# A fused two-block transformer step: the gate projection is spread over the attention steps, and a matmul sequence is grouped by shape

## The chip, the cores and the metric

The kernel runs on one NeuronCore of a Trainium2 chip. The metric is device time in microseconds for one execution, from start to end on that core. The engines named below are PE (TensorE, the matmuls; its weight loads are listed apart as PEld), ACT (ScalarE), DVE (VectorE), POOL (GpSimd) and SP (the queue that issues the weight DMAs).

## What is computed

Two transformer blocks run on 256 tokens of width 1024, all in fp32. The change touches only the mixing layer of the first block. Cut to what matters there:

```python
h = _rms_norm(x, mix_norm)
proj = h @ w_in                      # 256 x 1024 times 1024 x 3584
aq, ak, av, hq, hf, hi, hg = split(proj)      # each 512 wide
attn_out = _dilated_attention(rope(norm(aq)), rope(norm(ak)), av)   # 8 heads of 64
rec = _hgrn2(hq, hf, hi, lower_bounds)        # 4 heads of 128, chunks of 64 tokens
rec = _rms_norm(rec, hg_out_norm) * silu(hg)  # the gate
x = x + concat([attn_out, rec]) @ w_out
```

The recurrence's output for a chunk is a masked 128x128 product with its values plus the decayed queries times the state before the chunk: `(intra + inter)`.

## The kernel before, in words

Every matrix of weights is cut into blocks of 128 x 2048 floats (1 MB). SP streams them in the order of a list, `plan` (lines 190 to 245), into a ring of eight slots; a slot is loaded again once the block that lay in it is used. A block is then split into a high part (ACT, line 299, `act_split`) and a low part (DVE, line 307, `dve_split`), so that an fp32 product becomes three fp32r matmuls (`mm3`, line 180). There are four slots for high parts, so a block can be split only when the block four places earlier in the list has been used. Each engine runs one program in a fixed order that is written out by hand, and the engines meet through semaphores alone.

A projection to 512 columns by `pe_tok` (line 528) takes two blocks, its halves. Each half is 24 matmuls of 512 columns (two token tiles, four k tiles, three products) into two PSUM banks. The five such projections have the numbers 0 (aq), 1 (ak), 2 (av), 3 (hi, the recurrence's values) and 4 (hg, the gate). In the list and on PE they stand in the order 0, 1, 3, 4, 2. ACT empties the banks in `kept` (line 794): a copy for 3 and 2, a silu for 4.

Between the halves of projections 4 and 2 stand small matmuls of the recurrence: `pe_rec_head` (line 637, per head the score product and two transposes), `pe_rec_state` (line 652, a chunk's state), and the transposes of q and k, `pe_qk_turn` (line 691).

Then the attention loop (line 749) runs over steps 0 to 10. A head h passes through these stations: `pe_scores` (PE) in step h; `biased` (DVE, line 917: bias and maximum) in step h; `exps` (ACT, line 805) in step h; `scaled` (DVE, line 927: division by the sum) in step h+1; `pe_turn_p` (PE, line 712, three transposes) in step h+2; `turned_p` (ACT, line 813, the copy out of PSUM) in step h+2; `pe_pv` (PE, line 723) in step h+3; and for each pair of heads `values` on ACT and on DVE. `pe_rec_out` (line 664) writes the recurrence's outputs in step 4 for both token tiles; `squares` on ACT (line 827) reads them in step 6 for both token tiles, and `roots`, `means` and `gated` follow. After the loop come the first group of `w_out` (24 matmuls, into banks 2 to 5), `pe_rec_turn` (line 677), and the groups 1 to 3 of `w_out`. ACT and DVE split the block of `w_out` 3 after their loops (lines 870 and 1001).

Plain fp32 matmuls, as in the attention and the recurrence, appear in the trace as two records each, called passes below.

Of the kernel before, what the change touches and what calls it, by code (L numbers as in the profile page):

```python
# [11 lines left out]
ACT = mybir.ActivationFunctionType  # L12
# [7 lines left out]
SPLIT = 4  # L20
# [72 lines left out]
def build(nc, a):  # L93
    ctx = ExitStack()
    with ctx:
# [81 lines left out]
        def mm(e, out, l, r, start, stop, **kw):  # L177
            return e.matmul(out, l, r, start=start, stop=stop, **kw)  # L178
# [6 lines left out]
        def both(x, f):  # L185
            return [f(y) for y in x]
# [22 lines left out]
        plan_ffn("ffn1", a["ffn1_w13"], a["ffn1_w2"], GROUPS)  # L209
        plan_all("w_hf", a["w_hf"])  # L210
        plan_all("w_hq", a["w_hq"])
        for i in (0, 1, 3, 4, 2):
            plan_all(("w_tok", i), a["w_tok"][i])
        plan_all("w_out", a["w_out"])
        plan_ffn("ffn2", a["ffn2_w13"], a["ffn2_w2"], GROUPS)
# [8 lines left out]
        for i in range(2):  # L224
# [10 lines left out]
            first = len(plan)  # L235
# [292 lines left out]
        def pe_tok(e, name, b0, b1, fresh=None, between=None):  # L528
            for half in range(2):
                blk, W = weights(e, (name, half), k=4)  # L530
                for t, b in ((0, b0), (1, b1)):
                    for k in range(4):
                        if fresh and t == 0 and k % 2 == 0:
                            e.wait_ge(*xt_low.at(fresh, 2 * half + k // 2))
                        i = mm3(e, banks[b][:, :], both(XT3, lambda x: x[:, 4 * half + k, t * 128:t * 128 + 128]),
                                both(W, lambda x: x[:, k, :]), half == 0 and k == 0, half == 1 and k == 3)
                    if half == 1 and t == 0:
                        i.then_inc(*half_done.mark(name))
                i.then_inc(*used.mark(blk))
                if half == 0 and between:  # L540
                    between()
# [90 lines left out]
        rec_att, rec_state, rec_out, rec_turned = signal("rec_att", mix_pe), signal("rec_state", mix_pe), signal("rec_out", mix_pe), signal("rec_turned", mix_pe)  # L632
        qk_turned, att_z, p_turned, att_v = signal("qk_turned", mix_pe), signal("att_z", mix_pe), signal("p_turned", mix_pe), signal("att_v", mix_pe)

        last_tok = index[("w_tok", 2), 1]

        def pe_rec_head(e, h):
            P = banks[h % 2]
# [25 lines left out]
        def pe_rec_out(e):  # L664
            for tt in range(2):
                P = banks[1 - tt]
                e.wait_ge(*state_n.at(2 if tt else 1))
                for h in range(4):
                    hv = slice(h * 128, h * 128 + 128)
                    i = mm(e, P[:, hv], att8[:, 2 * h + tt, :], HI3[:, tt, hv], True, False, skip_group_check=True)  # L670
                    for c in (2 * tt, 2 * tt + 1):
                        if c:
                            i = mm(e, P[(c % 2) * 64:(c % 2) * 64 + 64, hv], E1h[:, h, c * 64:c * 64 + 64],
                                   prv[:, c - 1, h, :], False, c % 2 == 1, skip_group_check=True)
                i.then_inc(*rec_out.mark(tt))
# [10 lines left out]
                i.then_inc(*rec_turned.mark(hp))  # L686

        def turned_bank(i, gp):
            return banks[(2 if i else 6) + gp]

        def pe_qk_turn(e, i):
            q3 = qk[i].rearrange("p (t d) -> p t d", t=2)
            e.wait_ge(*roped.at(i, 1))
            for gp in range(2):
                e.wait_ge(*(tok_kept.at(4, gp) if i else qk_norm.at(1, gp)))
                for k in range(2):
                    for t in range(2):
                        g = 2 * gp + k
                        j = e.transpose(turned_bank(i, gp)[:, k * 256 + t * 128:k * 256 + t * 128 + 128],
                                        q3[:, t, g * 128:g * 128 + 128], ident)  # L700
                j.then_inc(*qk_turned.mark(i, gp))
# [21 lines left out]
        def pe_pv(e, h):  # L723
            P, p = banks[6 + h // 2 % 2], PT[h % NP]
            o_, hv = slice((h % 2) * 64, (h % 2) * 64 + 64), slice(h * 64, h * 64 + 64)
            e.wait_ge(*pt_kept.at(h))
            if h >= 4 and h % 2 == 0:
                e.wait_ge(*mix_low.at("pv", h // 2 - 2))
            mm(e, P[o_, 0:128], V3[:, 0, hv], p[:, 0:128], True, True)
            mm(e, P[o_, 128:256], V3[:, 0, hv], p[:, 128:256], True, False)  # L730
            mm(e, P[o_, 128:256], V3[:, 1, hv], p[:, 256:384], False, True).then_inc(*att_v.mark(h))

        def pe_mix(e):
            pe_proj(e, ("w_hf", 0), XT3, banks[0], "mix")
            pe_proj(e, ("w_hf", 1), XT3, banks[1])
            pe_proj(e, ("w_hq", 0), XT3, banks[2])
            pe_proj(e, ("w_hq", 1), XT3, banks[3])
            pe_tok(e, ("w_tok", 0), 4, 5)
            pe_tok(e, ("w_tok", 1), 6, 7)
            e.wait_ge(*forget.at(1))  # L740
            pe_tok(e, ("w_tok", 3), 0, 1)
            e.wait_ge(*q_dec.at(1))
            pe_tok(e, ("w_tok", 4), 2, 3, between=lambda: (pe_rec_head(e, 0), pe_rec_head(e, 1)))
            pe_rec_head(e, 2)
            pe_rec_head(e, 3)
            pe_qk_turn(e, 0)
            e.wait_ge(*qk_norm.at(0, 1))
            pe_tok(e, ("w_tok", 2), 4, 5, between=lambda: (pe_rec_state(e, 0), pe_qk_turn(e, 1)))
            for i in range(11):
                if i < 8:  # L750
                    pe_scores(e, i)
                if i < 2:
                    pe_rec_state(e, 1 + i)
                elif i == 4:
                    pe_rec_out(e)
                if 2 <= i <= 9:
                    pe_turn_p(e, i - 2)
                if i >= 3:
                    pe_pv(e, i - 3)
            e.wait_ge(*mix_low.at("pv", 1))  # L760
            pe_down(e, "w_out", XT3, range(1), 2)
            pe_rec_turn(e)
            e.wait_ge(*mix_low.at("pv", 3))
            pe_down(e, "w_out", XT3, range(1, 2), 2)
            e.wait_ge(*mix_low.at("rec", 1))
            pe_down(e, "w_out", XT3, range(2, 4), 2)

        def act_mix(e, c):
# [25 lines left out]
            def kept(i, b, buf, func):  # L794
                for t in range(2):
                    tok_done(e, ("w_tok", i), t)
                    e.activation(buf[:, t * 512:t * 512 + 512], banks[b + t][:, :], func).then_inc(*tok_kept.mark(i, t))
# [26 lines left out]
                e.wait_ge(*att_masked.at(h))  # L824
                e.copy(ksT[:, h * 256:h * 256 + 256], banks[h % 2][:, 256:512]).then_inc(*ks_kept.mark(h))

            def squares():
                for tt in range(2):
                    e.wait_ge(*rec_out.at(tt))
                    for h in range(4):  # L830
                        hv = slice(h * 128, h * 128 + 128)
                        i = e.activation(XN3[:, tt, hv], banks[1 - tt][:, hv], ACT.Square,
                                         accum_out=rss[:, 4 * tt + h:4 * tt + h + 1])
                i.then_inc(*rec_sq.mark())

            def roots():
                e.wait_ge(*rec_mean.at())
# [6 lines left out]
                                 scale=par("hgn")).then_inc(*mix_high.mark("rec", hp))  # L844
            act_split(e, c, index[("w_tok", 3), 0] + SPLIT)
            kept(3, 0, HI, ACT.Copy)
            act_split(e, c, index[("w_tok", 4), 0] + SPLIT)
            kept_head(0)
            kept_head(1)
            kept(4, 2, SHG, ACT.Silu)  # L850
            kept_head(2)
            kept_head(3)
            turned_qk(0, -0.125)
            act_split(e, c, index[("w_tok", 2), 0] + SPLIT)
            e.wait_ge(*rec_state.at(0))
            e.copy(prev[:, 0:512], banks[0][:, :]).then_inc(*state_0.mark())
            turned_qk(1, 1.0)
            kept(2, 4, V, ACT.Copy)
            for i in range(12):
                if i < 8:  # L860
                    exps(i)
                if 2 <= i <= 9:
                    turned_p(i - 2)
                if i >= 5 and i % 2:
                    values((i - 5) // 2)
                if i == 6:
                    squares()
                elif i == 8:
                    roots()
            act_split(e, c, last_tok + SPLIT)  # L870
            rec_xt()
            for g in range(3):
                act_split(e, c, index["w_out", g] + SPLIT)
# [1 line left out]
        def dve_mix(e, c):  # L875
# [82 lines left out]
                i.then_inc(*state_n.mark(n))  # L958

            def means():  # L960
                e.wait_ge(*rec_sq.at())
                e.tensor_scalar(rss, rss, 1.0 / 128, 1e-6, ALU.mult, ALU.add).then_inc(*rec_mean.mark())

            def gated():
# [16 lines left out]
            dve_split(e, c, index[("w_tok", 3), 0] + SPLIT)  # L981
            masked(0)
            masked(1)
            dve_split(e, c, index[("w_tok", 4), 0] + SPLIT)
            masked(2)
            masked(3)
            dve_split(e, c, index[("w_tok", 2), 0] + SPLIT)
            for i in range(12):
                if i < 8:
                    biased(i)  # L990
                if 1 <= i <= 8:
                    scaled(i - 1)
                if i >= 5 and i % 2:
                    values((i - 5) // 2)
                if i in (1, 2):
                    states(i)
                elif i == 7:
                    means()
                elif i == 9:
                    gated()  # L1000
            dve_split(e, c, last_tok + SPLIT)
            rec_xt()
            for g in range(2):
                dve_split(e, c, index["w_out", g] + SPLIT)
# [1490 lines left out]
```

## Time and profile before

| what | value |
|---|---|
| median of 3 runs | 1333.2 us (1331.91 to 1340.69) |
| the profiled execution's own time | 1335.28 us |
| its span in the trace | 1333.4 us |
| granted PE clock over the span | 0.983 of full speed |
| PE busy | 1269.5 us, 95% of the span |
| DVE, ACT, POOL busy | 612.2, 466.9, 205.6 us |
| chain that ended last | PE 89%, DVE 7%, ACT 2% |

The span is the time from the first to the last instruction in the trace; the time of the execution is 1.9 us more. The chain is followed back from the last instruction, at each step to what released it. An engine that is off this chain can be late without cost until another engine waits for it. The mixing layer lies between about 220 and 350 us of the span; the stretch that the change reorders lies between 270.56 and 333.51 us.

### The profile page before, as it was taken

How to read it: one execution, taken by the hardware profiler on the slowest of the kernel's cores; microseconds unless marked ns; L12 is line 12 of the kernel's file. 1: busy time of each engine (PE TensorE's matmuls, PEld its weight loads, DVE VectorE, ACT ScalarE, POOL GpSimd, SP SyncE). 2: the span in 40 equal slices, each digit the busy share in tenths (PEclk: the TensorE clock that was granted, in tenths of full speed). 3: DMA queues.
4: the chain of work that ended last, by engine and by line, in shares of the span. 5: the costliest groups of instructions: out<-in, count | busy, mean ns of one | idle time of the engine just before them, and what ended most of it. 6: DMA issues, size and time to landing. Idle time of an engine off the chain costs nothing.

```text
span 1333.4 us, 18498 instructions
## 1 busy us (share of the span) xinstructions
PE 1269.5 (95%) x7906; PEld 924.0 (69%) x7906; DVE 612.2 (46%) x816; ACT 466.9 (35%) x634; POOL 205.6 (15%) x207
## 2 busy tenths in 40 slices
PE   6999999998999999999899999997999899999995
PEld 6999997886799999888664444434898665444432
DVE  6644556845676764476731111117465651111114
ACT  5544344655446444325410101014676420001111
POOL 0000000410499990030000000000033000000000
PEclk9999999999999999989999999998999999999998
DMA  9555553540555555515599999996523399999992
GB/s 390 185 180 180 186 190 129 191 159 28 174 185 187 190 189 167 190 41 188 200 373 419 422 421 420 421 421 248 169 92 127 127 350 395 421 421 421 421 420 113
DMA packets 47750, 338.33 MB, mean 254 GB/s; under 512 B 5296, under 2 KB 5296, under 8 KB 7728
## 3 DMA queue, kind: packets, MB, share of 16 engines
q1 hardware_dynamic: 45936, 330.53, 64.6%
q10 hardware_dynamic: 1728, 6.55, 1.3%
q8 instruction: 66, 1.08, 0.3%
q14 instruction: 20, 0.16, 0.0%
HBM read 336.02 MB, written 1.05 MB: 253 GB/s over the span
## 4 chain that ended last, share of the span: by engine, by line
PE 89%; DVE 7%; ACT 2%; issue 1%; DMA 1%; SPq 0%; ACTq 0%; DVEq 0%
PE pb L178 88%; DVE halves L307 1%; DVE SM L1476 1%; DVE Xs L1487 1%; DMA ring<-in_ffn_w 1%; PE pb L1916 1%; DVE Xs L403 0%; DVE Xs L1482 0%; DVE Xs L405 0%; DVE XN L340 0%; ACT halves L299 0%; DVE p L1655 0%; DVE XN L349 0%; DVE Xs L1500 0%; DVE XTl L392 0%
## 5 line engine op out<-in xcount | busy, mean ns | idle before, releaser
L178 PE MATMUL pb<-XTh,halves 128*128 128x256 f32 x1856 | 338.8, 283 | 6.9 <-DVE XTl L392 4.9
L307 DVE TENSOR_TENSOR halves<-ring,halves 128x2048 fp32r<-128x2048 f32 (+1 forms) x122 | 285.1, 2352 | 130.2 <-ACT halves L299 129.9
L178 PEld LDWEIGHTS pb<-XTh,halves 128*128 128x128 f32 x1856 | 291.2, 192 | 9.1 <-issue 4.1
L178 PE MATMUL pb<-XTl,halves 128*128 128x256 f32 x928 | 262.3, 283 | 0.0
L299 ACT CAST halves<-ring 128x2048 fp32r<-128x2048 f32 (+1 forms) x122 | 227.4, 1874 | 83.4 <-PE pb L178 79.4
L178 PE MATMUL pb<-ring,gather 128*64 128x512 f32 x832 | 189.8, 598 | 3.2 <-DVE gather L2054 1.7
L178 PEld LDWEIGHTS pb<-XTl,halves 128*128 128x128 f32 x928 | 177.8, 192 | 0.9
L178 PE MATMUL pb<-halves,XTh 128*128 128x512 f32 x512 | 160.5, 395 | 5.0 <-DVE halves L307 3.0
L178 PEld LDWEIGHTS pb<-ring,gather 128*64 128x64 f32 x832 | 57.5, 137 | 109.2 <-issue 105.0
L2050 DVE TENSOR_TENSOR slots_h<-slots_silu,pb 128x256 f32<-128x256 f32 x32 | 13.5, 421 | 229.3 <-ACT slots_silu L2012 229.3
L178 PEld LDWEIGHTS pb<-halves,XTh 128*128 128x128 f32 x512 | 95.6, 190 | 26.0 <-DVE halves L307 6.0
L178 PE MATMUL pb<-halves,HTh 128*128 128x512 f32 x352 | 110.8, 396 | 0.0
L178 PE MATMUL pb<-halves,XTl 128*128 128x512 f32 x256 | 100.0, 391 | 0.0
L2058 DVE SCALAR_TENSOR_TENSOR slots_y<-pb,SM,slots_y 128x512 fp32r<-128x512 f32 x32 | 24.0, 751 | 117.4 <-ACT slots_y L2024 117.4
L178 PEld LDWEIGHTS pb<-places,XN 128*128 128x128 f32 x512 | 60.1, 193 | 23.4 <-issue 23.4
L1679 POOL TENSOR_TENSOR p<-p,CO 128x256 f32<-128x256 f32 x16 | 14.9, 959 | 392.1 <-DVE p L1659 392.1
L2024 ACT ACTIVATE slots_y<-pb,SM 128x512 fp32r<-128x512 f32 x32 | 22.0, 688 | 152.2 <-PE pb L178 152.2
L178 PEld LDWEIGHTS pb<-halves,HTh 128*128 128x128 f32 x352 | 64.8, 188 | 14.1
L178 PE MATMUL pb<-ring,slots_ht 128*64 128x512 f32 x320 | 72.9, 597 | 0.0
L178 PE MATMUL pb<-halves,HTl 128*128 128x512 f32 x176 | 69.6, 395 | 0.0
L178 PE MATMUL pb<-places,XN 128*128 128x128 f32 x512 | 65.8, 283 | 1.6 <-ACT gate_sig L1840 1.6
L2016 ACT COPY slots_ht<-pb 128x256 f32<-128x256 f32 x32 | 11.9, 372 | 138.4 <-PE pb L1916 138.0
(348 smaller groups left out, 1389.4 us busy)
## 6 DMA issues: line engine op xcount, KB each, us to landing
ring<-in_moe_w SPq DMA_DIRECT2D x144, 1024.0 KB, 13.6
ring<-in_ffn_w SPq DMA_DIRECT2D x66, 1024.0 KB, 5.0
extra<-in_moe_w SPq DMA_DIRECT2D x48, 1024.0 KB, 14.6
ring<-in_w_tok SPq DMA_DIRECT2D x10, 1024.0 KB, 5.0
ring<-in_ple_gate SPq DMA_DIRECT2D x8, 1024.0 KB, 4.9
ring<-in_w_out SPq DMA_DIRECT2D x4, 1024.0 KB, 4.9
ring<-in_ab_out SPq DMA_DIRECT2D x4, 1024.0 KB, 4.9
ring<-in_sb_v SPq DMA_DIRECT2D x4, 1024.0 KB, 22.8
```

What stands on the lines that cost most here:

```text
L178: return e.matmul(out, l, r, start=start, stop=stop, **kw)
L299: e.copy(split_of(n)[0], raw_of(n)).then_inc(*high.mark(n))
L307: e.tensor_tensor(l, raw_of(n), h.bitcast(F32), ALU.subtract).then_inc(*low.mark(n))
L1476: s = e.bn_stats(st4[:, t, h, :], X3[:, t, h * 512:h * 512 + 512])
L1487: e.scalar_tensor_tensor(x, x, r, GB[:, 1024:2048], ALU.mult, ALU.add).then_inc(*x_new.mark("norm", i, t))
L1679: e.tensor_tensor(diag(LL[h % 8]), diag(LL[h % 8]), strict2, ALU.mult).then_inc(*sb_strict.mark(h))
L1916: j = e.transpose(banks[7][:, c * 128:c * 128 + 128], HM[n][:, c * 128:c * 128 + 128], ident)
L2016: e.copy(HT4[p % 2][:, 2 * n:2 * n + 2, :], banks[7][:, 0:256]).then_inc(*s.h_kept.mark(p, n))
L2024: e.activation(Y[h][0], down_bank(p, h)[:, :], ACT.Copy, scale=slot_gate[:, p:p + 1]).then_inc(*s.y_high.mark(p, h))
L2050: e.tensor_tensor(HM[n], SL[n], banks[5 + n][:, 256:512], ALU.mult).then_inc(*s.mul.mark(p, n))
L2058: e.scalar_tensor_tensor(Y[h][1], down_bank(p, h)[:, :], slot_gate[:, p:p + 1], Y[h][0].bitcast(F32), ALU.mult, ALU.subtract).then_inc(*s. ...
```

## The change

The list of blocks and PE's order have the values' projection (2) before the gate's (4). The gate's 48 matmuls are no longer issued by `pe_tok` but by a new function, `pe_gate`, in four portions: 8 before `pe_rec_state(0)`, then 13, 13 and 14 in the attention steps 0, 1 and 2. They write banks 6 and 7. The transposes of q use banks 2 and 3 as those of k do. In `pe_rec_out` the four heads' masked products are issued first, then the products with the state. It is called in step 3 in place of 4. ACT applies silu in step 3, takes the squares of the first token tile in step 3 and of the second in step 8, and the roots in step 10. The splits of later blocks move into steps 1 and 3 on ACT and 0, 1 and 3 on DVE. The last two `pe_pv` are issued after the first group of `w_out`, which now has a wait for each bank.

```diff
-        for i in (0, 1, 3, 4, 2):
+        for i in (0, 1, 3, 2, 4):
             plan_all(("w_tok", i), a["w_tok"][i])
...
-                    i = mm(e, P[:, hv], att8[:, 2 * h + tt, :], HI3[:, tt, hv], True, False, skip_group_check=True)
+                    mm(e, P[:, hv], att8[:, 2 * h + tt, :], HI3[:, tt, hv], h == 0, False, skip_group_check=True)
+                for h in range(4):
+                    hv = slice(h * 128, h * 128 + 128)
                     for c in (2 * tt, 2 * tt + 1):
...
         def turned_bank(i, gp):
-            return banks[(2 if i else 6) + gp]
+            return banks[2 + gp]
...
-                e.wait_ge(*(tok_kept.at(4, gp) if i else qk_norm.at(1, gp)))
+                e.wait_ge(*(qkt_kept.at(0, gp) if i else q_dec.at(1)))
...
-            if h >= 4 and h % 2 == 0:
-                e.wait_ge(*mix_low.at("pv", h // 2 - 2))
+            if h % 2 == 0:
+                e.wait_ge(*(tok_kept.at(4, h // 2) if h < 4 else mix_low.at("pv", h // 2 - 2)))
...
+        def pe_gate(e, first, stop):
+            for n in range(first, stop):
+                half, t, k, part = n // 24, n // 12 % 2, n // 3 % 4, n % 3
+                blk, W = index[("w_tok", 4), half], both(split_of(index[("w_tok", 4), half]), lambda x: x.rearrange("p (k n) -> p k n", k=4))
+                if n % 24 == 0:
+                    e.wait_ge(*low.at(blk))
+                if half == 0 and k == 0 and part == 0:
+                    e.wait_ge(*qk_norm.at(1, t))
+                i = mm(e, banks[6 + t][:, :], XT3[part == 2][:, 4 * half + k, t * 128:t * 128 + 128], W[part == 1][:, k, :],
+                       half == 0 and k == 0 and part == 0, half == 1 and k == 3 and part == 2)
+                if n % 24 == 23:
+                    i.then_inc(*used.mark(blk))
+                elif n == 35:
+                    i.then_inc(*half_done.mark(("w_tok", 4)))
...
-            e.wait_ge(*q_dec.at(1))
-            pe_tok(e, ("w_tok", 4), 2, 3, between=lambda: (pe_rec_head(e, 0), pe_rec_head(e, 1)))
+            e.wait_ge(*qk_norm.at(0, 1))
+            pe_tok(e, ("w_tok", 2), 4, 5, between=lambda: (pe_rec_head(e, 0), pe_rec_head(e, 1), pe_qk_turn(e, 0)))
             pe_rec_head(e, 2)
             pe_rec_head(e, 3)
-            pe_qk_turn(e, 0)
-            e.wait_ge(*qk_norm.at(0, 1))
-            pe_tok(e, ("w_tok", 2), 4, 5, between=lambda: (pe_rec_state(e, 0), pe_qk_turn(e, 1)))
-            for i in range(11):
+            pe_qk_turn(e, 1)
+            pe_gate(e, 0, 8)
+            pe_rec_state(e, 0)
+            for i in range(10):
                 if i < 8:
                     pe_scores(e, i)
-                if i < 2:
-                    pe_rec_state(e, 1 + i)
-                elif i == 4:
+                if i in (1, 2):
+                    pe_rec_state(e, i)
+                elif i == 3:
                     pe_rec_out(e)
+                if i < 3:
+                    pe_gate(e, 8 + 13 * i, 21 + 13 * i if i < 2 else 48)
                 if 2 <= i <= 9:
                     pe_turn_p(e, i - 2)
-                if i >= 3:
+                if 3 <= i < 9:
                     pe_pv(e, i - 3)
             e.wait_ge(*mix_low.at("pv", 1))
-            pe_down(e, "w_out", XT3, range(1), 2)
+            pe_down(e, "w_out", XT3, range(1), 2, free=lambda b: att_max.at(6 + b) if b < 2 else pt_kept.at(4 + b))
+            pe_pv(e, 6)
+            pe_pv(e, 7)
             pe_rec_turn(e)
```

On ACT, in order (DVE's splits stand beside them in steps 0, 1 and 3):

```diff
-            act_split(e, c, index[("w_tok", 4), 0] + SPLIT)
+            act_split(e, c, index[("w_tok", 2), 0] + SPLIT)
             kept_head(0)
             kept_head(1)
-            kept(4, 2, SHG, ACT.Silu)
+            turned_qk(0, -0.125)
+            kept(2, 4, V, ACT.Copy)
             kept_head(2)
             kept_head(3)
-            turned_qk(0, -0.125)
-            act_split(e, c, index[("w_tok", 2), 0] + SPLIT)
+            turned_qk(1, 1.0)
             e.wait_ge(*rec_state.at(0))
             e.copy(prev[:, 0:512], banks[0][:, :]).then_inc(*state_0.mark())
-            turned_qk(1, 1.0)
-            kept(2, 4, V, ACT.Copy)
+            act_split(e, c, index[("w_tok", 2), 1] + SPLIT)
             for i in range(12):
                 if i < 8:
                     exps(i)
+                if i == 1:
+                    act_split(e, c, index[("w_tok", 4), 0] + SPLIT)
+                elif i == 3:
+                    kept(4, 6, SHG, ACT.Silu)
+                    act_split(e, c, index[("w_tok", 4), 1] + SPLIT)
+                    squares(0)
                 if 2 <= i <= 9:
                     turned_p(i - 2)
                 if i >= 5 and i % 2:
                     values((i - 5) // 2)
-                if i == 6:
-                    squares()
-                elif i == 8:
+                if i == 8:
+                    squares(1)
+                elif i == 10:
                     roots()
-            act_split(e, c, last_tok + SPLIT)
             rec_xt()
```

## Rows read from the trace of the kernel before

**Rows 1.** The page: busy time of each engine, and the chain that ended last.
```profile
PE 1269.5 (95%) x7906; PEld 924.0 (69%) x7906; DVE 612.2 (46%) x816; ACT 466.9 (35%) x634; POOL 205.6 (15%) x207
...
PE 89%; DVE 7%; ACT 2%; issue 1%; DMA 1%; SPq 0%; ACTq 0%; DVEq 0%
```

**Rows 2.** Timeline of PE: start us, us, operation; in brackets the idle before.
```profile
270.56 0.61 PE L178 MATMUL pb<-halves,XTh 128*128 128x512 f32 x2
...
276.00 0.60 PE L178 MATMUL pb<-p,p 128*128 128x128 f32 x4
...
298.13 2.83 PE L178 MATMUL pb<-p,p 64*128 64x128 f32 x28
301.97 0.55 PE L720 MATMUL pb<-CO,p 128*128 128x128 f32 x3 [1.01 <-DVE p L933]
...
304.21 0.55 PE L720 MATMUL pb<-CO,p 128*128 128x128 f32 x3 [0.85 <-DVE p L933]
304.92 7.99 PE L178 MATMUL pb<-p,p 128*64 128x128 f32 x50 [0.17 <-ACT p L817]
312.85 0.55 PE L720 MATMUL pb<-CO,p 128*128 128x128 f32 x3
...
314.97 0.55 PE L720 MATMUL pb<-CO,p 128*128 128x128 f32 x3
...
319.80 0.87 PE L178 MATMUL pb<-p,p 128*64 128x128 f32 x6
...
323.11 1.45 PE L178 MATMUL pb<-p,p 128*64 128x128 f32 x6 [1.88 <-ACT p L817]
324.57 0.90 PE L720 MATMUL pb<-CO,p 128*128 128x128 f32 x3
...
327.12 0.73 PE L178 MATMUL pb<-halves,XTh 128*128 128x512 f32 x2
...
333.51 0.70 PE L178 MATMUL pb<-halves,XTh 128*128 128x512 f32 x2
```

**Rows 3.** Busy time by stretch: engines in order, PEclk, DMA share, GB/s.
```profile
306.57:312.85 6.28, 6.28 (x42) 3.94 (x41) 1.28 (x8) 1.72 (x7) 0.00 (x0) 1.00 0.00 0
...
323.10:327.12 4.02, 4.00 (x21) 3.10 (x21) 1.91 (x8) 2.85 (x6) 0.00 (x0) 0.58 0.00 0
```

**Rows 4.** Timeline of PE's weight loads in attention step 4.
```profile
305.72 0.52 PEld L178 LDWEIGHTS pb<-p,p 64*128 64x128 f32 x4 [0.17 <-issue]
...
308.91 0.61 PEld L178 LDWEIGHTS pb<-p,p 128*128 128x128 f32 x4 [0.17 <-issue]
309.69 0.62 PEld L178 LDWEIGHTS pb<-p,p 128*128 128x128 f32 x6 [0.17 <-issue]
```

**Rows 5.** Busy time by stretch, one microsecond after PE's last wait.
```profile
324.00:325.00 1.00, 0.99 (x5) 0.59 (x4) 0.52 (x2) 1.00 (x1) 0.00 (x0) 0.50 0.00 0
```

**Rows 6.** Timeline of ACT: the loop's start, head 2, head 4.
```profile
298.85 1.28 ACT L808 ACT_TABLE_LOAD   x1
300.14 0.40 ACT L808 ACTIVATE p<-p,SM 128x128 f32<-128x128 f32 x1
...
303.52 0.40 ACT L808 ACTIVATE p<-p,SM 128x128 f32<-128x128 f32 x1 [1.52 <-DVE SM L924]
...
304.41 0.46 ACT L817 COPY p<-pb 128x384 f32<-128x384 f32 x1
...
307.35 0.40 ACT L808 ACTIVATE p<-p,SM 128x128 f32<-128x128 f32 x1
```

**Rows 7.** Groups of ACT's instructions, 276 to 333.51 us: count, busy us, mean ns.
```profile
L299 ACT CAST halves<-ring 128x2048 fp32r<-128x2048 f32 x4 | 7.6, 1910 | 5.8 <-PE pb L178 5.8
...
L797 ACT ACTIVATE p<-pb 128x512 f32<-128x512 f32 x4 | 2.4, 598 | 5.9 <-PE pb L178 5.9
...
L832 ACT ACTIVATE XN<-pb 128x128 f32<-128x128 f32 x8 | 2.1, 291 | 0.0
```

**Rows 8.** Timeline of DVE: the low part of one block.
```profile
292.65 2.29 DVE L307 TENSOR_TENSOR halves<-ring,halves 128x2048 fp32r<-128x2048 f32 x1 [2.31 <-ACT halves L299]
```

More of the change, by code:

```diff
@@ L633, in build @@
         qk_turned, att_z, p_turned, att_v = signal("qk_turned", mix_pe), signal("att_z", mix_pe), signal("p_turned", mix_pe), signal("att_v", mix_pe)
-        last_tok = index[("w_tok", 2), 1]
+        last_tok = index[("w_tok", 4), 1]
         def pe_rec_head(e, h):
@@ L825, in kept_head, with squares @@
                 e.copy(ksT[:, h * 256:h * 256 + 256], banks[h % 2][:, 256:512]).then_inc(*ks_kept.mark(h))
[L827 to L834, printed above, removed]
+            def squares(tt):
+                e.wait_ge(*rec_out.at(tt))
+                for h in range(4):
+                    hv = slice(h * 128, h * 128 + 128)
+                    i = e.activation(XN3[:, tt, hv], banks[1 - tt][:, hv], ACT.Square,
+                                     accum_out=rss[:, 4 * tt + h:4 * tt + h + 1])
+                i.then_inc(*rec_sq.mark(tt))
             def roots():
@@ L960, in means @@
             def means():
-                e.wait_ge(*rec_sq.at())
+                e.wait_ge(*rec_sq.at(1))
                 e.tensor_scalar(rss, rss, 1.0 / 128, 1e-6, ALU.mult, ALU.add).then_inc(*rec_mean.mark())
@@ L983, in dve_mix @@
             masked(1)
-            dve_split(e, c, index[("w_tok", 4), 0] + SPLIT)
+            dve_split(e, c, index[("w_tok", 2), 0] + SPLIT)
             masked(2)
             masked(3)
-            dve_split(e, c, index[("w_tok", 2), 0] + SPLIT)
             for i in range(12):
@@ L994, in dve_mix @@
                     values((i - 5) // 2)
-                if i in (1, 2):
-                    states(i)
-                elif i == 7:
+                if i == 0:
+                    dve_split(e, c, index[("w_tok", 2), 1] + SPLIT)
+                elif i == 1:
+                    states(1)
+                    dve_split(e, c, index[("w_tok", 4), 0] + SPLIT)
+                elif i == 2:
+                    states(2)
+                elif i == 3:
+                    dve_split(e, c, index[("w_tok", 4), 1] + SPLIT)
+                elif i == 9:
                     means()
-                elif i == 9:
+                elif i == 10:
                     gated()
-            dve_split(e, c, last_tok + SPLIT)
             rec_xt()
```

## The prediction, made before the changed kernel was run

> **What bounds the kernel now.** I read the page first. PE is busy 95% of the span and holds 89% of the chain that ended last [rows 1]: a change pays only if it takes work or idle time from PE, and work that is only moved on PE pays nothing. The changed code lies between 270.56 us (first half of projection 4) and 333.51 us (group 1 of `w_out`), 62.95 us or 4.7% of the span, so the whole effect has to be found there. PE's timeline of this stretch [rows 2] shows four things that are not work at full speed.
>
> 1. Waits at the loop's start: 1.01, 0.85 and 0.17 us, while heads 0 and 1 go through DVE and ACT and PE has nothing else to issue.
> 2. `pe_rec_out`, from 306.57 to 312.85 us: 6.28 us for 40 passes [rows 3]. Its weight loads show why. A head with 4 passes takes 0.78 us from start to start, a head with 6 also (309.69 less 308.91), and each time 0.17 us of nothing stand ahead of the next head [rows 4]. Each head alternates between a product that fills 128 columns of the array and products that fill 64.
> 3. One wait of 1.88 us at 323.11, for the copy of head 5's transposed probabilities on ACT, which stands behind all eight squares in ACT's queue.
> 4. A low clock behind that wait: 0.58 granted from 323.10 to 327.12 [rows 3], and 0.50, the 1.2 GHz level, in a whole microsecond of it [rows 5]. Six passes of `pe_pv` take 1.45 us there and 0.87 us before it, three transposes 0.90 and 0.55 [rows 2].
>
> **The change part by part.** I follow PE's order with these durations up to the start of `w_out` group 1, and keep ACT's and DVE's queues beside it.
>
> *Projections swapped.* Both have two halves of 24 matmuls, 5.44 us each (276.00 less 270.56, [rows 2]), 0.227 us a matmul. The swap costs nothing on PE. The transposes of q move in between the halves; their rotation by POOL was needed earlier than that in neither kernel, since q's projection is the first of the five.
>
> *The gate's 48 matmuls.* 10.9 us of PE work, moved and not removed. With about 0.11 us a pass, two heads take 1.3, the transposes of q or k 0.8, a chunk's state 1.1: from 276.0 on, 1.3 + 0.8 + 5.4 + 1.3 + 0.8 + 1.8 (8 gate matmuls) + 1.1 bring PE to step 0 at about 288.6 us (298.13 before). Steps 0 to 2 add 40 gate matmuls (9.1), three scores, two states and the changes of shape (4.0): the gate is issued at 301.6. PE doesn't idle until then: heads 0 and 1 have three portions of about 3 us as cover. This removes the 2.03 us of item 1. The cover matters, since ACT now casts a block (1.91 us, [rows 7]) and loads Exp's table (1.28, [rows 6]) before head 0's exponentials; these start at about 292.4, head 0's transposes only at 301.6. The cost: the portions are a shape of their own between the 64-row products of scores and states, which stood together (28 passes in one run at 298.13). Three more changes of shape each way at 0.17 us at most [rows 4], less where the next load is hidden: I take 0.5 us, bounds 0 and 1.0.
>
> *`pe_rec_out` grouped.* 16 changes of shape become 4. With 0.17 us a change and two passes of 128 columns at 0.11, a head of 0.78 us leaves 0.22 us for its four 64-column passes; pairs at different columns seem to overlap, as heads with 4 and 6 passes take the same. Grouped: token tile 0 is 8 + 8 passes and 2 changes, 2.1 us; tile 1 is 8 passes, 8 pairs and 2 changes, 2.3. Sum 4.4, so 1.9 us saved. Bounds: 0 if the order within a bank doesn't matter, 2.3 if all is hidden.
>
> *ACT in step 3.* This is the new place to be late. After head 3's exponentials (scores at 302.1, 1.63 us later as for head 4, 305.72 to 307.35, [rows 4, 6], and 0.89 us long, 303.52 to 304.41) ACT is at 304.6. Behind them stand: Silu's table 1.28, two silus 1.1 (0.60 each, overlapping a little, [rows 7]), the cast of `w_out` 3 1.85, four squares 1.0 (half of the 2.0 us from 319.65 on; the group row has 2.1), and only then the copy of head 1's transposes: ready to start at 309.8, done at 310.3. PE asks for it, in `pe_pv(1)`, after 301.6 + 0.5 + 0.85 + 4.4 + 0.5 + 0.8 + 0.85 + 0.5 = 310.0 (transposes 0, scores 3, outputs, transposes 1, `pe_pv(0)`, scores 4, transposes 2; the loop's period of 2.12 us, 312.85 to 314.97, [rows 2], is made of 0.48, 0.80 and 0.85). Wait: 0.3 us. DVE stands behind ACT's cast with its own 2.29 us [rows 8], so head 4's maximum comes at 311.7; Exp's table is back at 311.5. Heads 3 and 4 are late by this, and PE waits 0.6 us more at `pe_turn_p(3)`, 0.3 at 6 (heads 5 to 7 follow DVE and ACT closely) and 0.7 at 7.
>
> *Squares and last values.* With the squares halved and the second half behind head 6's copy, the 1.88 us of item 3 go. The last two `pe_pv` stand behind 24 matmuls of `w_out`, which hide their copies; then 0.1 us is left before group 1. The four bank waits of `w_out` 0 cost nothing: bank 4 is asked for 1.4 us into it. Without the wait of 1.88 us the low clock goes as well: 0.6 + 0.35 us in the two rows of item 4, 1.0 us in all; bounds 0 (it falls anyway) and 1.0.
>
> *DMA.* The loads released by the two halves of the block that now comes last go out at about 295 and 301.6 (290.5 and 298.1 before); the DMA engines are idle from 306 to 327 [rows 3], and these loads are for ffn2, after 358 us. Nothing.
>
> *Sum.* 2.03 + 1.88 idle, 1.9 grouping, 1.0 clock, less 0.5 for shapes and 2.0 for new waits: 4.3 us. Followed step by step, group 1 of `w_out` starts at 329.2 in place of 333.51. Behind it the order is the same and PE bound, so the gain stays. Against the profiled time of 1335.28 that is 1331.0; that execution stands 2.1 us above the median of 1333.2, and I give the prediction for the median: **1329.0 us**.
>
> One dependence is worth saying: ACT's queue sets `pe_pv(1)`. If grouping saved nothing, PE would come 1.9 us later and not wait there, and the end would be only 0.9 us later. If PE were faster still, ACT would eat it.
>
> **A rule of the Trainium skill against the trace.** The table load of 1.28 us at 298.85 is followed by its exponential at 300.14, 1.29 us later, with nothing between [rows 6]. The Trainium skill (ScalarE: Activation LUTs, What ACT_TABLE_LOAD costs) has a drain of 1.38 us beside the load, 2.66 us for each switch. By it the sum would be 1.8 us in place of 4.3. The trace doesn't agree.
>
> **The rivals.**
> - *Forecast* (0.66): 1329.0, own range 1326.5 to 1331.5.
> - *No new waits* (0.10): ACT and DVE keep up in step 3. Then 6.3 us are gained: 1326.9. For it: item 1's removal leaves heads ahead. Against: the queue in step 3 is counted from rows.
> - *Table switches at double price* (0.08): the change adds one switch (Exp, Silu, Exp, Sqrt for Silu, Exp, Sqrt) and moves two into step 3, between head 3 and head 4. If the load's own 1.28 us stood once more behind each of them, head 1's copy would be done at 311.6 and head 4's exponentials would start at 314.1, 2.4 us later than forecast; two of these reach PE: a gain of 2.0 us, 1331.2. The load at 298.85 speaks against it [rows 6]; it might hold where more is in flight on ACT before the load.
> - *Slower, by the clock* (0.05): the new waits lie close together from 310 to 320 us. A wait of 1.88 us did drop the clock; 1.01 and 0.85 didn't. If it fell at 310 and stayed at 1.2 GHz to the end of `w_out` 0, some 9 us of attention work would take 1.65 times as long (1.45 for 0.87) and 5.4 us of matmuls twice, less 2 us of waits that vanish in it: +9.3, net 5 us slower, 1338. It decides from about 10 us of low clock on (4.3 + 2 over 0.65); before it lasted about 4.
> - *The change doesn't do what it says* (0.05): the gate's operands come late and PE waits inside the portions. Then item 1's gain and cover are gone and some 1 us stays: 1332. The split of the gate's second block ends at about 280 (DVE) and is needed at 295, so 15 us speak against it.
> - *Something outside the stretch* (0.06), either sign, such as another place of code or data in memory: nothing in the profile shows it; half of it is for more than 13 us faster and half for more than 13 us slower.
>
> **The numbers.** What a measurement of this kernel can tell from no change is about 1%, 13 us; only the last case gets there. So faster 0.03, within 1% 0.94, slower 0.03. The range takes the forecast's own, the rivals from 1326.9 to 1332, and the spread of a median of runs that themselves go from 1331.91 to 1340.69: 1325.0 to 1334.0.
>
> **What would show it.** PE without a wait over 0.3 us until the gate is issued; `pe_rec_out` at 4.4 us with few gaps ahead of its weight loads; ACT without idle between head 3's exponentials and head 1's copy; no wait near 1.9 us before `w_out`, and the clock at 1.00 through the loop; `w_out` 1 at about 329 us. Wrong would be: `pe_rec_out` still above 5.5, a gap behind a table load, or a wait over 1.5 us at `pe_pv(1)` with the clock falling behind it.

## The result, and the profile after

| | kernel before | changed kernel |
|---|---|---|
| median, executions in turns | 1340.41 us (1331.23 to 1343.65, 21 executions) | 1328.08 us (1326.45 to 1331.29, 21 executions) |
| span of the profiled execution | 1333.4 us | 1326.1 us |
| the stretch, from the first `pe_rec_head` to group 1 of `w_out`, in the profiled execution | 57.51 us | 53.62 us |

The ratio of the times is 0.9922, 95% interval 0.9906 to 0.9939. The forecast was 1329.0, range 1325.0 to 1334.0: the time lies in it. But the kernel before was itself at 1340.41 in this larger set, and not at the 1333.2 of the three executions shown: the difference is 12 us, almost three times the 4.3 that were forecast. Much of what follows is about these 8 us.

The changed stretch first, as PE's timeline of the changed kernel has it (start us, us, operation, idle before it; the rows without `halves` from the loop's third step to head 3's value product, those with a wait behind them, and the marks at both ends).

```profile
277.38 0.61 PE L178 MATMUL pb<-p,p 128*128 128x128 f32 x4
...
304.11 0.49 PE L722 MATMUL pb<-CO,p 128*128 128x128 f32 x3
304.53 5.14 PE L178 MATMUL pb<-p,p 64*128 64x128 f32 x44
309.60 0.55 PE L722 MATMUL pb<-CO,p 128*128 128x128 f32 x3
310.07 1.72 PE L178 MATMUL pb<-p,p 128*64 128x128 f32 x10
311.72 0.55 PE L722 MATMUL pb<-CO,p 128*128 128x128 f32 x3
312.80 1.72 PE L178 MATMUL pb<-p,p 128*64 128x128 f32 x10 [0.53 <-ACT p L838]
314.92 0.55 PE L722 MATMUL pb<-CO,p 128*128 128x128 f32 x3 [0.40 <-DVE p L957]
315.64 1.72 PE L178 MATMUL pb<-p,p 128*64 128x128 f32 x10 [0.18 <-ACT p L838]
...
321.59 0.87 PE L178 MATMUL pb<-p,p 128*64 128x128 f32 x6 [0.17 <-ACT p L838]
322.98 0.55 PE L722 MATMUL pb<-CO,p 128*128 128x128 f32 x3 [0.51 <-DVE p L957]
...
331.00 0.73 PE L178 MATMUL pb<-halves,XTh 128*128 128x512 f32 x2
```

This execution began 1.38 us later (277.38 for the 276.00 of [rows 2]), so durations are compared, not times. The waits of 1.01, 0.85 and 1.88 us in [rows 2] are gone. Scores 3 and the recurrence's outputs take 5.07 us together (304.53 to 309.60), so the outputs some 4.2, where they took 6.28 [rows 3]. In place of the old waits stand 0.53, 0.40, 0.18, 0.17 and 0.51 us, 1.8 in all, the first two of them at the places that the forecast named: `pe_pv(1)` and `pe_turn_p(3)`.

ACT's timeline of the changed kernel in step 3, which answers to [rows 6]:

```profile
306.96 0.19 ACT L831 ACTIVATION_READ_ACCUMULATOR p<-p,SM 128x1 f32 x1
307.16 1.28 ACT L818 ACT_TABLE_LOAD   x1
308.45 1.08 ACT L818 ACTIVATE p<-pb 128x512 f32<-128x512 f32 x2
309.43 1.90 ACT L299 CAST halves<-ring 128x2048 fp32r<-128x2048 f32 x1
311.21 0.29 ACT L852 ACTIVATE XN<-pb 128x128 f32<-128x128 f32 x1
...
312.23 0.51 ACT L838 COPY p<-pb 128x384 f32<-128x384 f32 x1
312.76 1.28 ACT L829 ACT_TABLE_LOAD   x1
314.24 0.40 ACT L829 ACTIVATE p<-p,SM 128x128 f32<-128x128 f32 x1 [0.19 <-DVE SM L948]
```

ACT has no idle time from head 3's exponentials to the copy of head 1's transposes at 312.23, for which PE waits. The silus follow 1.29 us after the start of their table load, at once behind it; the work of the second load waited 0.19 us for DVE (head 4's maximum). The drain of 1.38 us that the Trainium skill has beside the load (ScalarE: Activation LUTs, What ACT_TABLE_LOAD costs) is not here either.

The rest of the difference of 7.3 us between the two spans lies 230 us further on, in the small products of the state-space layer. The kernel before, by stretch (busy time of PE, PEld, DVE, ACT, POOL, then PEclk, DMA share, GB/s), and the first matmul behind that layer (the row's last part but one is the start of the first and of the last):

```profile
565.00:568.00 3.00, 3.00 (x76) 3.00 (x71) 0.00 (x0) 0.00 (x0) 0.00 (x0) 0.60 0.42 172
568.00:571.00 3.00, 3.00 (x64) 3.00 (x64) 0.00 (x0) 0.00 (x0) 0.00 (x0) 0.50 0.03 5
...
577.00:580.00 3.00, 3.00 (x23) 2.18 (x16) 2.73 (x5) 1.15 (x2) 1.97 (x2) 0.63 0.00 0
...
L178 PE MATMUL pb<-places,XN x512: 275/275/422, 676.6 to 1280.4; 128*128 128x128 f32 x171
```

The changed kernel:

```profile
565.00:568.00 3.00, 3.00 (x100) 2.87 (x96) 0.08 (x1) 0.00 (x0) 0.00 (x0) 1.00 0.03 5
568.00:571.00 3.00, 3.00 (x70) 2.59 (x63) 2.93 (x7) 1.15 (x2) 0.00 (x0) 1.00 0.02 5
...
L178 PE MATMUL pb<-places,XN x512: 275/275/561, 669.2 to 1273.1; 128*128 128x128 f32 x171
```

From group 1 of `w_out` to that matmul it is 343.1 us before (676.6 less 333.51) and 338.2 after. So the spans differ by 3.9 us from the changed stretch and 4.9 from a spell at half the clock that this execution of the kernel before had and this one of the changed kernel had not, less 1.4 for the later start, which is itself a low clock (0.78 granted from 15 to 20 us of the span, where the trace of the kernel before has 1.00). These 4.9 us are in no line that was changed, and the next section shows that the 12 us between the medians are yet another sum.

### The profile page after: what moved, and what is told of

Read it like the earlier page. It is cut to its first block, busy times and chain, and to the rows that moved or that the text cites. A ratio compares the mean times of both kernels' runs of the same rounds, so it can differ in the third digit from the quotient of the medians.

```text
span 1326.1 us, 18501 instructions
## 1 busy us (share of the span) xinstructions
PE 1262.8 (95%) x7906; PEld 920.1 (69%) x7906; DVE 612.2 (46%) x816; ACT 468.6 (35%) x635; POOL 206.0 (16%) x207
## 4 chain that ended last, share of the span: by engine, by line
PE 88%; DVE 8%; ACT 1%; issue 1%; DMA 1%; SPq 0%; ACTq 0%; DVEq 0%
PE pb L178 87%; DVE halves L307 1%; DVE SM L1505 1%; DVE Xs L1516 1%; DMA ring<-in_ffn_w 1%; PE pb L1945 1%; DVE Xs L403 0%; DVE Xs L1511 0%; ACT halves L299 0%; DVE Xs L405 0%; DVE XN L340 0%; DVE p L1684 0%; PE pb L364 0%; DVE Xs L1529 0%; DVE rot L1404 0%
```

## The experiments

Two theories stood against each other. The **local** one is the forecast's: waits and passes in the changed stretch, at full clock, are all there is. The **clock** one: most of the difference is how often and how long PE's clock is at 1.2 GHz. All the medians below are of 7 to 12 executions, taken in turns with the kernel before, which had a median of 1340.3 to 1340.5 each time. They come from three chips. Such a median depends on how many executions happen to fall into the long group, as the first run shows, so the lists of times are compared too.

**The kernel before again** (no edit).

> The kernel before, unchanged, once more with a trace. Two theories on the 7.3 us between the two traces' spans. Local theory: what the change does in its own stretch (270.56 to 333.51 us) is all there is, about 4 us; then the executions of the kernel before differ among themselves for no reason that its trace shows, and the ratio to itself is 1.000 within 0.3%. Clock theory: about 4 us come from the stretch and the rest from PE's clock later on: in the trace of before it was at 1.2 GHz from about 565 to 579 us (the small products of the state-space layer), in the trace after it was not. Then executions of this kernel fall into groups (about 1332 and 1341), and the mean granted clock of an execution is lower in the long group, by some 0.005 to 0.01.

Measured: median 1334.95, for 1340.34 of the 35 executions of the same kernel beside it, ratio 0.9984 (0.9955 to 1.0012). Five of its 12 executions at 1340.4 to 1342.1 us with a granted clock of 0.977 or 0.978, seven at 1331.8 to 1335.3 with 0.983 to 0.987. Of the 35, 22 lay at 1339.3 to 1344.0 (0.976 to 0.981) and 13 at 1328.8 to 1335.4 (0.985 to 0.991); nothing between. The one that was profiled is of the long group, span 1340.0. Its PE timeline:

```profile
277.39 0.60 PE L178 MATMUL pb<-p,p 128*128 128x128 f32 x4
...
303.35 0.55 PE L720 MATMUL pb<-CO,p 128*128 128x128 f32 x3 [1.01 <-DVE p L933]
...
305.59 0.90 PE L720 MATMUL pb<-CO,p 128*128 128x128 f32 x3 [0.84 <-DVE p L933]
306.43 13.92 PE L178 MATMUL pb<-p,p 128*64 128x128 f32 x50
320.27 0.90 PE L720 MATMUL pb<-CO,p 128*128 128x128 f32 x3
...
336.04 0.55 PE L720 MATMUL pb<-CO,p 128*128 128x128 f32 x3
...
338.38 0.73 PE L178 MATMUL pb<-halves,XTh 128*128 128x512 f32 x2
...
344.75 0.71 PE L178 MATMUL pb<-halves,XTh 128*128 128x512 f32 x2
```

and its stretches:

```profile
304.00:315.00 11.00, 10.16 (x34) 6.22 (x34) 5.06 (x27) 3.68 (x14) 0.00 (x0) 0.53 0.01 2
315.00:325.00 10.00, 10.00 (x41) 6.14 (x41) 0.71 (x5) 0.54 (x2) 0.00 (x0) 0.50 0.00 0
325.00:335.00 10.00, 10.00 (x36) 6.76 (x35) 4.13 (x21) 6.59 (x33) 0.00 (x0) 0.50 0.01 2
...
335.00:340.00 5.00, 4.80 (x29) 3.73 (x29) 2.63 (x11) 4.13 (x7) 0.00 (x0) 0.95 0.01 2
```

The clock falls at the second of the two waits at the loop's start and stays at 1.2 GHz for some 30 us. It is back at 335.4 us, among the same small passes of the loop (the transposes at 336.04 take 0.55 us again), 3 us before the first matmul of `w_out` at 338.38. The wait of 1.88 us near the end is not in this execution; behind the second of the two waits PE waits only once more, for 0.20 us at 337.58. The 50 passes that took 7.99 us in [rows 2] take 13.92. The stretch is 67.36 us (344.75 less 277.39) for 57.51. So the 9 us between the groups are here, in the stretch that was changed, and the execution that the forecast was read from was one without the fall. This also turns the question: the state-space layer had no spell in this execution, and the clock theory's place was wrong.

**Grouping alone**, in the kernel before.

```diff
-                    i = mm(e, P[:, hv], att8[...], HI3[...], True, False, skip_group_check=True)
+                    mm(e, P[:, hv], att8[...], HI3[...], h == 0, False, skip_group_check=True)
+                for h in range(4):
+                    hv = slice(h * 128, h * 128 + 128)
```

> The kernel before with the recurrence's outputs grouped by shape and nothing else. Forecast's step: the outputs take 4.4 us for 6.28, and as every engine waits for PE there, group 1 of w_out starts 1.9 us earlier relative to the first half of projection 4 (62.95 us before, 61.1 expected). Rival: the saving becomes a longer wait before the copy of head 5 (1.88 us before), because ACT's eight squares are what that wait is made of; then under 0.5 us is left. Times of whole executions: 1331 or 1339, by the group that they fall into; under the clock theory both groups still occur.

```profile
304.98 5.94 PE L178 MATMUL pb<-p,p 128*64 128x128 f32 x50 [0.17 <-ACT p L819]
310.85 0.55 PE L722 MATMUL pb<-CO,p 128*128 128x128 f32 x3
...
321.12 0.87 PE L178 MATMUL pb<-p,p 128*64 128x128 f32 x6 [1.88 <-ACT p L819]
322.58 0.55 PE L722 MATMUL pb<-CO,p 128*128 128x128 f32 x3 [0.59 <-DVE p L935]
```

In PE's timeline the same 50 passes take 5.87 us to the next row (310.85 less 304.98) and took 7.93 (312.85 less 304.92, [rows 2]): 2.06 us for 12 changes of shape fewer, 0.17 each. The Trainium skill says that a change of tiling mode, not of tile, drains the engine (TensorEngine Tiling (Array Packing), Key Properties); the trace agrees in so far as each change costs time, 0.17 us; a drain as such is no row of it. 1.3 us of it reach the end of the stretch (56.21 us), for the 1.9 expected, in the main since a wait of 0.59 appears at head 7; the rival's 0.5 is out too. The median is 1335.16 with groups at 1329.2, 1334 to 1336.5 and 1338. The three at 1338, with a granted clock of 0.980 or 0.981, are probably the long group made 2 to 3 us shorter; none of them has a trace.

**The changed kernel without the grouping** (the same edit undone).

> The changed kernel with the recurrence's outputs in the old order within each token tile. Forecast's step: the outputs take 6.3 us, but the stretch grows only by 0.9 us, since ACT's queue in step 3 is what PE waits for behind them (the waits at head 1's and head 3's transposes shrink). Rival: no such cover, the stretch grows by the full 1.9 us. Clock theory: whole executions stay in the group of the changed kernel (1327 to 1332) if the gate's move is what keeps the clock up, and two groups come back if the outputs' grouping is.

Measured: stretch 54.37 us, 0.75 more than the changed kernel's, though the outputs took 2.05 us longer. No wait at heads 1 and 3 is left; they were what ACT's queue had cost. The cover is as forecast. Median 1329.71, but 3 of 12 executions at 1333.0 to 1335.5, where the changed kernel has none above 1331.43 in 28. There is no group at 1340, so the grouping is not what the changed kernel needs to be rid of it; what the three are has no trace.

**The changed kernel with squares and last values put back.**

```diff
-                    squares(0)                      # step 3
-                if i == 8:
-                    squares(1)
-                elif i == 10:
+                if i == 6:
+                    squares(0)
+                    squares(1)
+                elif i == 8:
                     roots()
...
-            pe_down(e, "w_out", XT3, range(1), 2, free=...)
-            pe_pv(e, 6)
-            pe_pv(e, 7)
+            pe_down(e, "w_out", XT3, range(1), 2)   # the values in steps 9 and 10
```

> The changed kernel with three things put back: squares of both token tiles in step 6 and roots and gating in steps 8 and 9 as before, and the last two value products ahead of w_out. Forecast's step: the wait near 1.9 us before head 5's value product comes back and the stretch grows by 1.6 us, by 2.6 if the clock falls behind the wait as it did before. Rival: heads are so far ahead after the gate's move that ACT's squares are hidden: under 0.5 us. Clock theory: if a low clock here is what leads to the low clock 240 us later, long executions (about 1338) come back.

```profile
315.06 0.55 PE L722 MATMUL pb<-CO,p 128*128 128x128 f32 x3 [1.00 <-DVE p L955]
...
322.99 0.87 PE L178 MATMUL pb<-p,p 128*64 128x128 f32 x6 [1.43 <-ACT p L836]
324.46 0.55 PE L722 MATMUL pb<-CO,p 128*128 128x128 f32 x3 [0.59 <-DVE p L955]
```

The stretch is 55.23 us, 1.61 more. PE's timeline has the wait at head 5 back, at 1.43 us. The clock did not fall here, and no long execution came (1329.5 to 1334.3): the wait near the end is not what makes the group at 1340. Nor does every pair of waits of this length bring the clock down: here are 1.00 and 1.43 us, 6.5 us apart, at a granted clock of 1.00 throughout.

**The two waits filled**, in the kernel before: one matmul that nobody reads ahead of the transposes of heads 0 and 1.

```diff
+                if i in (2, 3):
+                    mm(e, banks[7][:, :], ident, CO[:, 0:512], True, True)
                 if 2 <= i <= 9:
                     pe_turn_p(e, i - 2)
```

> The kernel before, with one matmul whose result nobody reads (0.9 us, into bank 7) put ahead of the transposes of head 0 and of head 1, where PE waits 1.01 and 0.85 us. Clock theory, as the traces now suggest it: these two waits are what lets PE's clock fall at about 305 us in most executions of the kernel before, and it then stays at 1.2 GHz for some 30 us. With the waits filled the group at 1340 us is gone; the median falls from 1340 to 1332 or 1333, with no useful work moved. Rival: the fall has another cause (the 64-row and 64-column products of the loop load the array too little), then the filling changes nothing: more than half of the executions stay above 1338, and the median is that of the kernel before.

```profile
298.00:304.00 6.00, 6.00 (x42) 4.17 (x40) 2.60 (x14) 3.74 (x10) 0.00 (x0) 1.00 0.51 176
304.00:315.00 11.00, 10.83 (x64) 6.63 (x65) 5.15 (x27) 3.77 (x15) 0.00 (x0) 1.00 0.00 1
```

Measured: median 1333.93, ratio 0.9960 (0.9936 to 0.9985), a little above the 1332 or 1333 expected, with a stretch of 57.57 us, which is the 57.51 of [rows 2]. Not one of 12 executions is at 1340; eleven lie at 1329.3 to 1337.2, one at 1354 (clock 0.933, not explained; the kernel before has one such too among its 25 beside it, at 1449.8 with 0.840). The traced one, at 1337.1, has the spell in the state-space layer. Adding useless work to PE (each filler takes 1.12 us in the trace) took 6.6 us off the median. This shows that the long group needs these two waits: with the same passes behind them, and no waits, it doesn't come. What it does not tell apart: a filler takes the idle time away and also puts a matmul of 512 columns among small ones, and either could be what holds the clock up. So do the gate's portions in the changed kernel.

**The gate's matmuls all ahead of the loop**, in the changed kernel.

```diff
-            pe_gate(e, 0, 8)
+            pe_gate(e, 0, 48)
             pe_rec_state(e, 0)
...
-                if i < 3:
-                    pe_gate(e, 8 + 13 * i, 21 + 13 * i if i < 2 else 48)
```

> The changed kernel with all 48 gate matmuls ahead of the recurrence's state 0 and none in the attention steps. Theory (the spread portions are cover): ACT's cast and table load now stand open, PE waits about 3 us at head 0's transposes and again about 3 us within the recurrence's outputs, the stretch grows by 7.5 us at full clock, and the clock falls behind these waits for a long spell, which adds up to 10 us: 1336 at the best, 1345 to 1350 in most executions. Rival (the gate's place is of no matter, the rest of the change carries the gain): the stretch grows by 2 us, the waits of the kernel before, 1330.

```profile
298.00:304.00 6.00, 3.19 (x29) 2.88 (x26) 4.18 (x13) 5.36 (x10) 0.00 (x0) 0.97 0.46 168
304.00:310.00 6.00, 6.00 (x23) 4.75 (x23) 4.71 (x14) 3.09 (x8) 0.00 (x0) 0.50 0.00 0
310.00:315.00 5.00, 3.57 (x34) 2.71 (x33) 2.00 (x11) 3.89 (x9) 0.00 (x0) 0.96 0.00 0
```

Measured: stretch 60.31 us, 6.7 more than the changed kernel's, for the 7.5 expected, with waits of 2.81, 0.52, 0.91 and 1.43 us as the largest; median 1337.83. The spread portions are the cover, though the second wait, within the outputs, is 0.52 us and not about 3. And the long spell did not come: the clock fell at 304 and was back at 310.4, before the second token tile's outputs (310.88). Nine executions are at 1334.5 to 1338.2 and three at 1342.9 to 1346.4; I had expected most above 1345. A fall is not yet a long spell; something else keeps the clock low.

**The same with the outputs in the old order.**

> The changed kernel with the gate's matmuls all ahead of the loop, and with the recurrence's outputs in the old order. With the gate first and the outputs grouped, PE's clock fell behind a wait of 2.81 us but was back at full speed some 6 us later, while in the long executions of the kernel before it stayed low for about 30 us. Theory G (the alternation of 128 and 64 columns is what keeps the clock low once it has fallen): the spell now lasts to the end of the loop and most executions come to 1345 us or more. Rival R (how long the spell lasts has to do with what follows the waits, not with the order within the outputs): 1 to 2 us longer than with the outputs grouped, median 1339 to 1340.

```profile
304.00:310.00 6.00, 5.98 (x18) 3.67 (x19) 4.72 (x13) 3.09 (x8) 0.00 (x0) 0.50 0.00 0
310.00:315.00 5.00, 5.00 (x20) 3.01 (x20) 2.04 (x11) 3.88 (x9) 0.00 (x0) 0.50 0.00 0
315.00:325.00 10.00, 10.00 (x39) 6.27 (x38) 3.56 (x8) 5.77 (x16) 0.00 (x0) 0.50 0.00 0
325.00:335.00 10.00, 10.00 (x36) 6.76 (x35) 4.22 (x22) 4.44 (x17) 0.00 (x0) 0.50 0.01 2
```

Behind the same wait of 2.81 us the clock now stays low to the end of the loop; the stretch is 69.65 us. Median 1343.16, nine of 12 at 1342.3 to 1350.4 where the grouped one had three. The median is a little under what I wrote (1345 or more), but the rival's 1339 to 1340 is out. So the order of the outputs probably has a hand in how long the clock stays down: one trace of each is not a law, and the share of executions (9 of 12 for 3 of 12, on two chips) is the firmer part. It can't be all of it. In this trace and in that of the kernel before again the clock stays at 0.50 through the loop steps behind the outputs, whose order no edit touched; and here too it comes back ahead of `w_out`: the last transposes, at 337.36 us, take 0.79 in place of 0.90, and `w_out` starts at 337.90. What brings the clock back is open.

**Both in the kernel before**: waits filled and outputs grouped, gate where it was.

> The kernel before with the two waits filled by a matmul each and the outputs grouped, the gate left where it was. If the clock's fall behind the waits is the greater part of the change's gain and the grouping adds 2 us to it, the median is 1330 to 1332, some 2 us under the filled kernel and 1 to 3 above the changed one, and no execution is above 1338. Theory G gives the same; a median above 1334 would say that filling and grouping don't add.

Measured: median 1330.41, ratio 0.9952 (0.9925 to 0.9979). Eight of 12 lie at 1327.8 to 1331.6, four at 1336.5 to 1337.0; the trace is of one of the four, its stretch is at full clock (54.81 us), and it has the spell in the state-space layer that the first trace had. The wait before head 5's value product stands in this stretch too, with 1.87 us, and the clock did not fall behind it; in the other three traces with that wait (the first one, grouping alone, waits filled) it did. The medians of the two kernels are 12.3 us apart; these two small edits bring 9.9 in this set.

**A lighter queue**: in the changed kernel the split of `w_out` 3 goes back behind the loops, the first squares go to the end of step 5, and head 7's transposes stand inside group 0 of `w_out`.

```diff
-                    act_split(e, c, index[("w_tok", 4), 1] + SPLIT)   # step 3; on DVE too
-                    squares(0)
+                if i == 5:
+                    squares(0)
...
+                        if hook and k == 0 and 2 * t + h == 1:
+                            hook()                                   # pe_turn_p(e, 7)
```

> The changed kernel with three waits attacked: the split of w_out 3 goes back behind the loops, the squares of the first token tile go from step 3 to the end of step 5, and the transposes of head 7 are issued inside w_out 0, after its first three matmuls. Theory (ACT's queue in step 3 and the thin steps at the end are what PE still waits for, 0.53 + 0.40 + 0.18 + 0.17 + 0.51 us): the stretch shrinks by 0.9 us and these waits go; whole executions 0.9 us shorter than the changed kernel, in the same groups. Rival: waits only move on along the heads, as DVE and ACT follow PE closely; under 0.3 us.

```profile
275.91 0.61 PE L178 MATMUL pb<-p,p 128*128 128x128 f32 x4
...
318.81 0.87 PE L178 MATMUL pb<-p,p 128*64 128x128 f32 x6 [0.17 <-ACT p L840]
...
327.70 0.72 PE L178 MATMUL pb<-halves,XTh 128*128 128x512 f32 x2
```

These are the stretch's two ends and the one wait that is left in it. It takes 51.79 us, 1.83 less than the changed kernel's 53.62: twice what I expected, since all but 0.17 of the 1.8 us of waits went. The 0.9 us expected of whole executions didn't come: median 1329.37 of 7, beside 1329.36 of 7 for the changed kernel. Seven executions of each that reach from 1322.95 to 1332.62 are too few to tell, as spells elsewhere move one by more.

**The changed kernel again**, on the same chip.

> The changed kernel once more, beside the others on the same chip. Both theories: median 1326.5 to 1331, no execution above 1336; granted clock 0.985 or more in all.

Measured: median 1329.36, 1326.8 to 1331.4, granted clock 0.986 to 0.989, stretch 53.62 us to the hundredth.

## Why the prediction was right, and where it was not

- *The two waits at the start.* Forecast 2.03 us gained, PE busy until the gate is issued: so it was, no wait in the first three steps.
- *Changes of shape in the outputs.* Forecast 1.9 us saved; grouping alone saves 2.06. That grouping alone would reach the end with only 0.9 us in the changed kernel: 0.75.
- *ACT in step 3.* The wait was forecast at `pe_pv(1)` with 0.3 us and at `pe_turn_p(3)` with 0.6; it was 0.53 and 0.40. Together with the later ones 2.0 was forecast and 1.8 found.
- *Changes of shape between the gate's portions.* Put at 0.5 us with a bound of 1.0; this term was mis-sized. PE is busy 53.55 of the stretch's 57.51 us before and 51.72 of 53.62 after, 1.8 less. The grouping (2.06) and the low clock behind the wait (0.58 and 0.35 us in the two rows of item 4) would make 3.0, so some 1.2 us are the price of the scattered portions, by difference.
- *Squares and last values.* The 1.88 us went; undone, 1.61 us come back, for the 1.6 expected. The low clock behind that wait, 1.0 us of the sum, is not in the changed kernel's trace; but it is no sure companion of the wait, as the fourth trace above has the wait without it.
- *Sum of the stretch.* 4.3 us forecast, 3.89 measured. The rivals are out: "no new waits" (they are there), the double price of the table switches (1.29 us from the load's start to the silus, and 1.30 at the loop's start, 292.78 to 294.08, in the changed kernel), the gate's operands late (no wait inside the portions), and slower by the clock. Something outside the stretch there was, but of 4.9 us and not of 13.
- *The step that failed*, though the time came out, is item 4 with its rival: "A wait of 1.88 us did drop the clock; 1.01 and 0.85 didn't." I read it from one execution. In most executions of the kernel before (22 of 35 in one set, 16 of 21 in that of the result) the time is that of the long group, and in the one of them with a trace the clock falls at these two waits, stays down for 30 us and costs 9.85 us (67.36 less 57.51). The clock's term was put at 1.0 us; for an average execution it is some 6 to 7 us more. In the 21 executions of the result the two groups' medians (1340.58 and 1331.91) lie 8.7 us apart: 3.9 + 16/21 x 8.7 = 10.5 us, and the ratio of 0.9922 is 10.5 us. I had the mechanism in the text, as a rival that would make the change slower, and missed that it was already at work in the kernel before.
- *The absolute time* came out right in part by luck. The local gain was taken from 1333.2, the median of three executions of which one, at 1340.69, was of the long group; and the changed kernel has only a short group. In the larger set 16 of 21 are long: with two long ones among the three the base would have been about 1340 and the forecast about 1336, 8 us above what was measured. The third time, 7.5 us above the others, was in the table and was read as spread. As a statement on the size of the gain, 0.3% for 0.8% was too small.
- Not settled: why the changed kernel and its variants have no spell in the state-space layer in any of their seven traces, while three of the five of the kernel before and its variants do (4.9 us in the one compared); why the same waits let the clock fall in some executions only; whether a filler works by the idle time that it takes away or by its own columns; and what ends a spell.

## What to carry to other kernels

Short idle times of PE between small products can cost five times their length (9.85 us for 1.01 and 0.84 here), if the clock falls in them and stays down behind them: price a wait of PE by what the clock does in many executions, not in the one with a trace. Look at the list of times first; two groups with nothing between them, with the granted clock lower in one, say that a profile shows one case of two. The cheapest test is to fill the wait with a matmul that nobody reads; if the time falls, real work moved there can pay twice, by the wait and by the clock.

## What the runs showed of the hardware

Behind waits of 1.01 and 0.84 us, 1.4 us apart, PE went to 1.2 GHz in one of two traces of the same kernel, and 22 of 35 executions have the time of that one; with one matmul in each wait no execution of 24 is in that group (one is at 1354, unexplained), and neither trace has the fall there. Once it was down it stayed down through 13.92 us of the recurrence's passes and some 15 us of attention passes, with PE busy throughout, and came back among such passes, 3 us ahead of the first matmul of `w_out`. A change between 128 and 64 columns costs 0.17 us (2.06 us for 12). The same kernel on the same chip gave 1328.8 to 1335.4 or 1339.3 to 1344.0 us and nothing between.
